# Norm weights spread from one row, Ln on the sum of squares, the sample's rows first, and first products on two tiles' columns

## The reference, cut to what matters

```python
def rms_norm(x, gain):
    xf = x.astype(jnp.float32)
    y = xf * lax.rsqrt(jnp.mean(xf * xf, axis=-1, keepdims=True) + NORM_EPS)
    return (y * gain.astype(jnp.float32)).astype(x.dtype)
...
hp = rms_norm(y_prompt, norm_pre[l])              # (1, 1024, 2048)
p = jnp.einsum('btd,de->bte', h, w_in)            # 56 tiles of 128 columns each
... three kinds of attention on slices of p, gated with silu(g) ...
y = y + rms_norm(jnp.einsum('btm,md->btd', mixed, w_out[l]), norm_post[l])
```

## Time and profile before

| | us |
|---|---|
| median of 3 runs (lowest to highest) | 1956.5 (1954.32 to 1958.09) |
| the profiled execution's own time | 1955.86 |
| its span in the profile | 1954.1 |
| PE busy | 1910.1 (98%) |
| DVE busy | 1218.0 (62%) |
| ACT busy | 673.6 (34%) |
| POOL busy | 53.7 (3%) |

### The profile page before, as it was taken

One profiled execution on the slowest core, in us unless ns is written; L12 is line 12 of the kernel. 1 busy time (PEld: TensorE's weight loads), 2 busy tenths in 40 slices (PEclk: granted clock), 3 DMA queues, 4 the chain that ended last, 5 costly groups with the idle time before them and its releaser, 6 DMA issues.

```text
span 1954.1 us, 31040 instructions
## 1 busy us (share of the span) xinstructions
PE 1910.1 (98%) x12604; PEld 1753.5 (90%) x12604; DVE 1218.0 (62%) x2172; ACT 673.6 (34%) x1261; POOL 53.7 (3%) x123
## 2 busy tenths in 40 slices
PE   5999999999999999999999999999999999999997
PEld 5999999999999999899999999989999988888875
DVE  7358777786868778453544454455435566866786
ACT  7124243343334334122222222223213354335554
POOL 3000000000000000000000000000000000000221
PEclk9999999999999999999999999999999999999998
DMA  6446777676776777566657666465446667556396
GB/s 243 116 119 138 157 157 161 145 157 146 151 156 148 164 156 152 112 149 136 151 119 151 140 139 139 107 137 127 102 93 141 140 218 261 193 177 219 120 264 162
DMA packets 879078, 301.04 MB, mean 154 GB/s; under 512 B 618424, under 2 KB 845512, under 8 KB 877352
## 3 DMA queue, kind: packets, MB, share of 16 engines
q1 hardware_dynamic: 875288, 288.25, 61.0%
q0 software_dynamic: 3648, 10.82, 2.8%
HBM read 210.45 MB, written 98.30 MB: 158 GB/s over the span
## 4 chain that ended last, share of the span: by engine, by line
PE 90%; DVE 4%; DMA 2%; issue 1%; ACT 1%; SPq 1%; POOL 0%; DVEq 0%; ACTq 0%; POOLq 0%
PE ps L1178 22%; PE ps L1179 21%; PE ps L1180 21%; PE ps L1389 4%; PE ps L1391 4%; PE ps L1390 4%; PE ps L1281 3%; PE ps L1360 3%; PE ps L1242 3%; PE ps L1331 3%; DMA b_out<-in_w_out_dram 1%; DVE arena L1722 1%; DVE act_lo L1729 1%; PE ps L1386 1%; PE ps L1385 1%
## 5 line engine op out<-in xcount | busy, mean ns | idle before, releaser
L1178 PE MATMUL ps<-act_hi,w_hi 128*128 128x352 f32 x2688 | 878.5, 327 | 3.9 <-DVE arena L1761 3.9
L1179 PE MATMUL ps<-act_lo,w_hi 128*128 128x352 f32 x2688 | 863.3, 321 | 0.0
L1180 PE MATMUL ps<-act_hi,w_lo 128*128 128x352 f32 x2688 | 863.3, 321 | 0.0
L1178 PEld LDWEIGHTS ps<-act_hi,w_hi 128*128 128x128 f32 x2688 | 505.1, 188 | 20.9 <-issue 18.1
L1179 PEld LDWEIGHTS ps<-act_lo,w_hi 128*128 128x128 f32 x2688 | 506.2, 188 | 0.0
L1180 PEld LDWEIGHTS ps<-act_hi,w_lo 128*128 128x128 f32 x2688 | 504.8, 188 | 0.0
L1492 ACT ACTIVATE w_hi<-w_raw 128x512 fp32r<-128x512 f32 x224 | 139.1, 623 | 350.0 <-DMA w_raw<-in_w_in_dram 349.8
L1737 DVE TENSOR_TENSOR w_lo<-w_raw,w_hi 128x512 fp32r<-128x512 f32 x224 | 150.6, 674 | 57.3 <-ACT w_hi L1492 57.0
L1559 ACT ACTIVATE arena<-arena,small 128x257 f32<-128x257 f32 (+6 forms) x180 | 101.2, 565 | 214.3 <-DVE small L1867 214.3
L2056 DVE STREAM_TRANSPOSE arena<-arena 128x1024 f32<-128x1024 f32 (+4 forms) x100 | 132.6, 1326 | 49.8 <-ACT arena L1680 49.0
L1680 ACT ACTIVATE arena<-arena 128x1024 f32<-128x1024 f32 (+1 forms) x60 | 61.0, 1017 | 251.0 <-DVE arena L1844 250.8
(11 more groups left out here) (182 smaller groups left out, 2101.4 us busy)
## 6 DMA issues: line engine op xcount, KB each, us to landing
w_raw<-in_w_in_dram SPq DMA_DIRECT2D x176, 256.0 KB, 3.4
weight_scratch<-arena SPq DMA_DIRECT2D x216, 128.0 KB, 3.5
arena<-weight_scratch SPq DMA_DIRECT2D x54, 512.0 KB, 4.5
b_out<-in_w_out_dram SPq DMA_DIRECT2D x72, 256.0 KB, 3.4
w_raw<-in_w_out_dram SPq DMA_DIRECT2D x70, 256.0 KB, 2.8
w_raw<-in_w_in_dram SPq DMA_DIRECT2D x96, 128.0 KB, 3.1
weight_scratch<-arena SPq DMA_DIRECT2D x80, 132.0 KB, 4.0
arena<-weight_scratch SPq DMA_DIRECT2D x40, 256.0 KB, 3.4
```

Source lines behind the costliest of these rows:

```text
L1178: mm(bank(g, GN), wh, ah, start=(k == 0), stop=False)
L1179: mm(bank(g, GN), wh, al, start=False, stop=False)
L1180: last = mm(bank(g, GN), wl, ah, start=False, stop=(k == KT - 1))
```

## The change

- **Norm weights.** One row of 2048 values is loaded (8 KB) instead of 128 copies of it (1 MB), as the first transfer. Four f32 matmuls of a column of ones (one partition high) by 512 of its values each spread it over 128 partitions in PSUM, and four copies on DVE bring it to `pre_gain`.
- **Ln.** The Ln takes the sum of squares itself, with scale 1/2048 and the epsilon as bias, and so no longer waits for POOL. POOL still makes the variance, for its Newton steps.
- **Order of the rows.** `ROWS` puts the sample's 32 rows first, then the eight prompt tiles. Row tiles are counted by their place in this order, `n`.
- **First products.** The products of the first weight tile are cut by columns: 256 columns of group 0 (two prompt tiles) after places 3 and 4 of the order, the other 96 after place 5, 288 of group 1 after 6 and 7, the other 64 after 8, then group 2 whole. Their number goes from 144 to 240. Later weight tiles are as before.

```diff
+ROWS = (TT,) + tuple(range(TT))
...
+        gain_row = place("gain_row", [1, D], F32, 0, ring0 + RING * PIECE)
+        ones_row = arena[0:1, 0:P]
+        eps_col = small[:, 149:150]
-        gain_in = sem("gain_in")
+        gain_in, gain_spread, gain_kept = sem("gain_in"), sem("gain_spread"), sem("gain_kept")
+        eps_made = sem("eps_made")
...
-            for t in range(TT + 1):
-                if t >= 4:
-                    sp.wait_ge(xt_done, 4 * (t - 4) + 4)
+            sp.dma_start(gain_row[:, :], norm_pre[0:1, :]).then_inc(gain_in, 16)
+            for n, t in enumerate(ROWS):
+                if n >= 4:
+                    sp.wait_ge(xt_done, 4 * (n - 4) + 4)
                 if t < TT:
-                    sp.dma_start(x_t[t % 4], x_prompt[0, P * t:P * t + P, :]).then_inc(x_in[t % 4], 16)
+                    sp.dma_start(x_t[n % 4], x_prompt[0, P * t:P * t + P, :]).then_inc(x_in[n % 4], 16)
                 else:
-                    sp.dma_start(x_t[t % 4][0:DEC, :], x_sample[0]).then_inc(x_in[t % 4], 16)
-                if t == 0:
-                    sp.dma_start(pre_gain, norm_pre[0].partition_broadcast(P)).then_inc(gain_in, 16)
-                if t == 3:
+                    sp.dma_start(x_t[n % 4][0:DEC, :], x_sample[0]).then_inc(x_in[n % 4], 16)
+                if n == 3:
                     for q in range(4):
                         in_piece(0, q)
...
-            def x_tile(t):
-                rows = rows_of(t)
...
                 for g in range(4):
-                    pe.wait_ge(x_norm, t + 1)
-                    if t:
-                        pe.wait_ge(x_lo, 4 * t + g - 3)
+                    pe.wait_ge(x_norm, n + 1)
+                    if n == 0:
+                        pe.wait_ge(gain_kept, g + 1)
+                    if n:
+                        pe.wait_ge(x_lo, 4 * n + g - 3)
...
-            def first_project(g, *quarters):
-                pe.wait_ge(x_lo, 4 * (3 * g + 3))
+            def first_product(g, q, a, b):
+                for kk in range(4):
+                    k = 4 * q + kk
+                    wh, wl = w_hi[:, q, P * kk:P * kk + P], w_lo[:, q, P * kk:P * kk + P]
+                    ah, al = act_hi[:, k, GN * g + a:GN * g + b], act_lo[:, k, GN * g + a:GN * g + b]
+                    out = bank(g, b - a, P, a)
+                    mm(out, wh, ah, start=(k == 0 and a == 0), stop=False, skip_group_check=True)
+                    mm(out, wh, al, start=False, stop=False, skip_group_check=True)
+                    last = mm(out, wl, ah, start=False, stop=(k == KT - 1), skip_group_check=True)
+                return last
+
+            def first_project(g, a, b, *quarters):
+                end = GN * g + b
+                pe.wait_ge(x_lo, 4 * (2 + (end - 1) // P) if end < TOK else 4 * (TT + 1))
                 for q in quarters:
                     pe.wait_ge(lo_made, q + 1)
-                    last = product(g, q)
-                    if q == 3:
+                    last = first_product(g, q, a, b)
+                    if q == 3 and b == GN:
                         last.then_inc(proj_done, 1)
                     elif g == GROUPS - 1:
                         last.then_inc(piece_used, 1)
+
+            EARLY_PARTS = {3: (0, 0, 2 * P, 0, 1), 4: (0, 0, 2 * P, 2, 3), 5: (0, 2 * P, GN, 0, 1, 2, 3),
+                           6: (1, 0, 5 * P - GN, 0, 1), 7: (1, 0, 5 * P - GN, 2, 3), 8: (1, 5 * P - GN, GN, 0, 1, 2, 3)}
...
+            pe.wait_ge(gain_in, 16)
+            pe.wait_ge(zeroed, 2)
+            for g in range(4):
+                mm(bank(X + g), ones_row, gain_row[:, PIECE * g:PIECE * g + PIECE], start=True, stop=True).then_inc(gain_spread, 1)
             pe.wait_ge(consts, CONSTS)
-            for t in range(TT + 1):
-                x_tile(t)
-
-                if t >= 3:
-                    first_project(t // 3 - 1, *((0,), (1, 2), (3,))[t % 3])
-            first_project(GROUPS - 1, 0, 1, 2, 3)
+            for n in range(TT + 1):
+                x_tile(n)
+                if n in EARLY_PARTS:
+                    first_project(*EARLY_PARTS[n])
+            first_project(GROUPS - 1, 0, GN, 0, 1, 2, 3)
...
+            def x_guess(n):
+                t = ROWS[n]
                 rows = rows_of(t)
-                r = std_x[0:rows, t % 3:t % 3 + 1]
-                act.wait_ge(x_var, t + 1)
-                fn(r, var[0:rows, t:t + 1], ACT.Ln).then_inc(x_ln, 1)
-                act.wait_ge(x_ln, t + 1)
+                r = std_x[0:rows, n % 3:n % 3 + 1]
+                act.wait_ge(x_sq, n + 1)
+                act.wait_ge(eps_made, 1)
+                fn(r, ssq[0:rows, t:t + 1], ACT.Ln, bias=eps_col[0:rows, :], scale=1.0 / D).then_inc(x_ln, 1)
+                act.wait_ge(x_ln, n + 1)
                 fn(r, r, ACT.Exp, scale=-0.5).then_inc(x_std, 1)
...
-
+            v.memset(ones_row, 1.0).then_inc(zeroed, 1)
+            v.memset(eps_col, EPS).then_inc(eps_made, 1)
+
+            def gain_copy(g):
+                dve.wait_ge(gain_spread, g + 1)
+                v.tensor_copy(pre_gain[:, PIECE * g:PIECE * g + PIECE], bank(X + g)).then_inc(gain_kept, 1)
+
+            for g in range(4):
+                gain_copy(g)
             dve.wait_ge(rel_in, 16)
             v.tensor_copy(ext[:, 0:P], tab[:, 2 * CLIP:2 * CLIP + 1].broadcast_to([H_C, P])).then_inc(ext_made, 1)
             v.tensor_copy(ext[:, P:P + 2 * CLIP], tab[:, 2 * CLIP - 1::-1]).then_inc(ext_made, 1)
-            dve.wait_ge(gain_in, 16)
...
+            def x_scale(n):
+                rows = rows_of(ROWS[n])
+                r = std_x[0:rows, n % 3:n % 3 + 1]
+                dve.wait_ge(x_rstd, 4 * n + 4)
+                dve.wait_ge(gain_kept, 4)
+                v.scalar_tensor_tensor(x_t[n % 4][0:rows, :], x_t[n % 4][0:rows, :], r, pre_gain[0:rows, :],
                                        ALU.mult, ALU.mult).then_inc(x_norm, 1)
...
-            for t in range(TT + 1):
+            for n, t in enumerate(ROWS):
...
-                pool.wait_ge(x_std, t + 1)
+                pool.wait_ge(x_std, n + 1)
+                pool.wait_ge(x_var, n + 1)
                 gp.tensor_tensor(nt, r, r, ALU.mult).then_inc(x_rstd, 1)
```

More of the change, by code:

```diff
@@ L1159, in _, with x_tile @@
             mm = nc.tensor.matmul
-            def x_tile(t):
-                rows = rows_of(t)
+            def x_tile(n):
+                rows = rows_of(ROWS[n])
                 for g in range(4):
-                    pe.wait_ge(x_norm, t + 1)
-                    if t:
-                        pe.wait_ge(x_lo, 4 * t + g - 3)
+                    pe.wait_ge(x_norm, n + 1)
[3 more added lines that the diff above has]
+                        pe.wait_ge(x_lo, 4 * n + g - 3)
                     for c in range(4):
                         last = nc.tensor.transpose(bank(X + g, rows, P, rows * c),
-                                                   x_t[t % 4][0:rows, P * (4 * g + c):P * (4 * g + c) + P],
+                                                   x_t[n % 4][0:rows, P * (4 * g + c):P * (4 * g + c) + P],
                                                    ident[0:rows, 0:rows])
@@ L1469, in _, with x_squares, x_high @@
             act.preload_act_table_set("natural_log_exp_and_others")
-            def x_squares(t):
+            def x_squares(n):
+                t = ROWS[n]
                 rows = rows_of(t)
-                act.wait_ge(x_in[t % 4], 16 * (t // 4 + 1))
-                fn(squares_x[0:rows, :], x_t[t % 4][0:rows, :], ACT.Square, accum_out=ssq[0:rows, t:t + 1]).then_inc(x_sq, 1)
-            def x_guess(t):
+                act.wait_ge(x_in[n % 4], 16 * (n // 4 + 1))
+                fn(squares_x[0:rows, :], x_t[n % 4][0:rows, :], ACT.Square, accum_out=ssq[0:rows, t:t + 1]).then_inc(x_sq, 1)
+            def x_guess(n):
+                t = ROWS[n]
                 rows = rows_of(t)
-                r = std_x[0:rows, t % 3:t % 3 + 1]
-                act.wait_ge(x_var, t + 1)
-                fn(r, var[0:rows, t:t + 1], ACT.Ln).then_inc(x_ln, 1)
-                act.wait_ge(x_ln, t + 1)
+                r = std_x[0:rows, n % 3:n % 3 + 1]
[3 more added lines that the diff above has]
+                act.wait_ge(x_ln, n + 1)
                 fn(r, r, ACT.Exp, scale=-0.5).then_inc(x_std, 1)
-            def x_high(t, g):
+            def x_high(n, g):
+                t = ROWS[n]
                 rows = rows_of(t)
-                act.wait_ge(xt_done, 4 * t + g + 1)
+                act.wait_ge(xt_done, 4 * n + g + 1)
                 fn(act_hi[:, 4 * g:4 * g + 4, P * t:P * t + rows],
@@ L1714, in _, with x_low @@
             v.tensor_copy(ext[:, P:P + 2 * CLIP], tab[:, 2 * CLIP - 1::-1]).then_inc(ext_made, 1)
-            dve.wait_ge(gain_in, 16)
[L1718 to L1722, removed]
+            def x_scale(n):
+                rows = rows_of(ROWS[n])
+                r = std_x[0:rows, n % 3:n % 3 + 1]
+                dve.wait_ge(x_rstd, 4 * n + 4)
+                dve.wait_ge(gain_kept, 4)
```

(21 more changed lines are left out.)

## The result

| | before | after |
|---|---|---|
| median of 6 runs, us | 1957.3 (1954.32 to 1959.94) | 1967.85 (1961.4 to 1969.59) |
| the profiled execution's own time, us | 1955.86 | 1969.59 |
| its span, us | 1954.1 | 1967.9 |
| end of the first weight tile on PE, us | 65.1 | 74.7 |

The change is slower: ratio 1.0046 (that of the two medians is 1.0054), 95% interval 1.0029 to 1.0064. Forecast were 1958.6 and at most 1962.8. The profiled execution lost 13.8 us of span, 9.6 of it before the first weight tile ends and 4.1 behind. For the kernel before that gives 65.1 (65.08), 0.1 more than the prediction's own sum of 65.0.

A forecast was written before the change was run, and what follows sets the result against it. PE was taken to bound the first weight tile: third scale 16.4, plus 14.6 + 0.1 + 2.2 + 33.8, ends it at 67.1, 2.1 later; 1955.9 + 2.1, plus 0.6 to the median, gives 1958.6 us. Range 1952.4 to 1962.8.

The forecast's parts named there:

- The head: Kernel start: norm-weight copies complete at 10.6 us, third scale at 16.4 (19.41 before), first products at 26 to 27.
- DVE up to place 4: DVE work from the third scale to the first low of prompt tile 2: 14.6 us, then PE turns place 4.
- S: Start of the third scale (prompt tile 1) on DVE: 16.4 us with a late head, 15.0 with an early one.
- Products of 256 and 288 columns: First weight tile on PE: 0.119 us a product at 256 columns and 0.133 at 288.
- 96 narrow products at 0.105: First weight tile: products of 96 or 64 columns, bound by the weight load at 0.105 us each, 10.1 us in all.
- E: End of the first weight tile on PE: 65.0 us before, forecast 67.1 after, 2.1 later.
- the plain f32 rate: Rival: short fp32r products take 0.165 us (96 columns) or 0.110 (64); first tile ends at 70.2, time 1961.7; chance 0.22.
- 0.069: Rival: short products don't wait for weights, 0.069 us each; first tile ends at 63.6, time 1955.1; chance 0.17.
- PE at the full clock from 31 us on: First weight tile: no idle PE from about 31 us, with wide products summed at full-clock pace and narrow ones at 0.105.
- The sum of 33.8 us: PE work after place 4's transposes: transposes of places 5 to 8 and the products to the first weight tile's end.
- A rule on the clock: First 24 products may run at half clock amid transposes: +1.1 us after 1.8 of spare time, 1959.7 instead of 1958.6.
- Behind E nothing new: After the first weight tile: no new waits; the second tile's weight load moves with that tile's end, so +2.1 us carries through.

The follow-up runs named there:

- 256-column run: The change with both rows of 48 narrow products made 256 columns wide, some columns added twice, so output not the reference's; 1962.98 us, ratio 1.0029 to the kernel before.
- whole-products run: The change with uncut 352-column products of groups 0 and 1, placed behind row places 4 to 8; 1958.62 us, ratio 1.0012 to the kernel before.

## Why the prediction was wrong

- *The head*: right. Copies end at 10.5 (forecast 10.6), third scale 16.57 (16.4), first product 27.27 (26 to 27).
- *DVE up to place 4*: right. S + 14.6 + 0.1 gives 31.1, place 4's transposes start at 31.38. The second sign of being wrong (PE waits for DVE behind 35 us) did not come, nor the third: the second tile didn't wait for its weights, as its first product starts at 74.71, right behind the last at 74.55, and its first `w_lo` at 72.45 (63.15 in the earlier trace rows).
- *Products of 256 and 288 columns*: right, 0.12 and 0.13.
- *96 narrow products at 0.105*: the direction right, the size 7% short. The distance is 0.112 at 96 and at 64 columns alike ((41.91 - 38.21)/33), so the columns don't count there. That is 0.7 us on E. The reason given, the weight load, fits a distance that stays the same from 64 to 192 columns, but no run changes the weight load alone. Of the rivals, the plain f32 rate fell with it (0.165 for 96 columns), and so did 0.069. The Trainium skill, "TensorE: Matmul & The Clock Gate", "Back-to-back issue gap", gives N/2.4 + 2.5 ns (43 and 29 ns here) for a matmul by itself, and says in the same place that this counts too little for short matmuls that each load weights, with some 81 ns at 128 columns. So the prediction's rival used the formula where that section doesn't; this trace has 112 ns at 128 columns, above both.
- *PE at the full clock from 31 us on*: this failed. The sum of 33.8 us took all its 216 products, the 96 narrow ones among them, at the full rate, with no term for the clock; "A rule on the clock" asked about the first 24 alone, because of the transposes ahead of them. Both falls came amid narrow products of a busy PE. They cost 6.8 us by the clock column. The 256-column run gives much the same by another way: the change's E less that run's, plus the 0.6 us that its wider products cost, is 74.7 - 69.0 + 0.6 = 6.3. With it the sum closes: 67.1 + 0.7 + 0.3 (place 4) + 6.3 to 6.8 = 74.4 to 74.9, measured 74.7. The low clock at 25 to 28 us, the one that was priced (+1.1), cost nothing: place 4's transposes start at 31.38 with it and, in the 256-column run, without it.
- No rival held a fall of the clock behind 31 us. The plain f32 rate had the right sign and 5.2 of the 9.6 us, by a mechanism that isn't there.
- *Behind E nothing new*: this failed too. 4.1 us came behind it in the first profile, 1.7 of them by the clock; the rest stays open.

The Trainium skill, "TensorE: Matmul & The Clock Gate", "HAM oscillation — how this bites in real kernels", sees the danger in gaps in which PE is idle. The whole-products run agrees (4.64 us of idle time, and 0.50 before they are over). The change's own falls have no gap in front of them (PE is busy for all of 31.4 to 42 us and 50 to 62 us), so keeping PE in work was not enough here.

## What to carry to other kernels

A cut that fills a wait with earlier, narrower matmuls has two prices: each piece costs at least the shortest distance between products (0.112 us here, with a new weight load each), and a long row of such pieces can bring the granted clock down to half while PE counts as 100% busy. Cut only as many as the wait needs and put wide products between: 180 for 240 products took E from 74.7 to 64.2 us (before: 65.1). Read the clock and the count per stretch, not the busy share, and take a second profile before a single fall is called fixed.

## What the runs showed of the hardware

- The granted clock fell to 0.50 amid fp32r products of 96 or 64 columns at 0.112 us apart, without idle time, in 8 of 9 rows of 48 (in one of them only with the last product); in the same places 48 products of 256 columns, at 0.12 apart, and in one profile 48 of 128 and 48 of 192, kept 1.00.
- fp32r products with a weight load of their own had a floor here: 0.112 us apart at 64, 96, 128 and 192 columns, 0.12 at 256.
- Four plain f32 matmuls of 512 columns with a stationary operand one partition high took 7.19 us as PE's first work, 1.8 each, twice the 0.88 of the earlier trace rows, while the clock column shows 1.00 for these first microseconds (2 to 12 us). The first 16 transposes of the kernel before were likewise at half pace (3.65 us for 1.91) at a column of 1.00, so at the very start the pace says more than the column.
